# Half-size block products in the two convolutional up stages: seven in place of eight

## The reference

```python
def conv_ffn(h, w_up, conv_w, w_down):
    g, u = jnp.split(dwconv(h @ w_up, conv_w), 2, axis=-1)
    return (jax.nn.silu(g) * u) @ w_down
```

## Time and profile before

| | us |
|---|---|
| median of three runs | 2925.28 |
| the profiled execution, whole | 2923.5 |
| its span in the trace | 2921.7 |
| PE busy | 2722.8 (93% of the span) |
| DVE busy | 575.8 (20%) |
| ACT busy | 356.4 (12%) |
| matmul line of the two up stages (L2830), busy | 455.3 |

### The profile page before, as it was taken

One profiled execution on the slowest core, in us unless ns is written; L12 is line 12 of the kernel. 1 busy time (PEld: TensorE's weight loads), 2 busy tenths in 40 slices (PEclk: granted clock), 3 DMA queues, 4 the chain that ended last, 5 costly groups with the idle time before them and its releaser, 6 DMA issues. The chain is left out here.

```text
span 2921.7 us, 70140 instructions
## 1 busy us (share of the span) xinstructions
PE 2722.8 (93%) x31522; PEld 1995.3 (68%) x31522; DVE 575.8 (20%) x1423; ACT 356.4 (12%) x896; POOL 85.7 (3%) x130
## 2 busy tenths in 40 slices
PE   6889999988899999999998898989999999898999
PEld 3758856658899899999896446865444444555883
DVE  0120001112000000001002224742222201232331
ACT  1010001001000000000002121221111100131110
POOL 0000000000000000000000002200000000000000
PEclk9999999989999999999998999999999999999999
DMA  8663435629999999999991110002222222302432
GB/s 348 258 248 146 156 130 204 257 87 342 364 405 417 392 407 420 411 402 419 400 418 76 43 72 30 3 2 72 79 80 72 72 87 79 119 18 83 148 144 86
DMA packets 80391, 583.94 MB, mean 200 GB/s; under 512 B 8912, under 2 KB 8912, under 8 KB 10064
## 3 DMA queue, kind: packets, MB, share of 16 engines
q1 hardware_dynamic: 79920, 580.15, 50.7%
q10 hardware_dynamic: 288, 1.05, 0.1%
HBM read 580.11 MB, written 1.05 MB: 199 GB/s over the span
## 5 line engine op out<-in xcount | busy, mean ns | idle before, releaser
L1471 PE MATMUL ps<-arena,ring 128*64 128x80 f32 x14336 | 509.5, 234 | 39.1 <-issue 36.1
L1471 PEld LDWEIGHTS ps<-arena,ring 128*64 128x64 f32 x14336 | 503.3, 138 | 44.6 <-issue 42.9
L2830 PE MATMUL ps<-hT,ring 128*128 128x256 f32 (+2 forms) x1472 | 455.3, 472 | 5.6 <-ACT hT L472 3.4
L2830 PEld LDWEIGHTS ps<-hT,ring 128*128 128x128 f32 x1472 | 274.5, 190 | 185.2 <-issue 166.3
L359 PE MATMUL ps<-ring,arena 128*128 128x512 f32 x896 | 390.7, 597 | 4.9 <-DVE arena L2735 3.8
L359 PEld LDWEIGHTS ps<-ring,arena 128*128 128x128 f32 x896 | 171.0, 192 | 218.4 <-issue 212.2
L1480 PE MATMUL ps<-arena,ring 128*64 128x80 f32 x7168 | 255.8, 234 | 19.4 <-issue 19.3
L1480 PEld LDWEIGHTS ps<-arena,ring 128*64 128x64 f32 x7168 | 251.9, 138 | 22.2 <-issue 21.9
L981 PE MATMUL ps<-hT,ring 128*128 128x256 f32 (+1 forms) x736 | 152.7, 370 | 2.6 <-ACT hT L470 2.6
L1621 DVE TENSOR_TENSOR arena<-arena,ps 128x80 f32<-128x80 f32 x224 | 53.2, 237 | 486.9 <-ACT arena L1600 486.8
L981 PEld LDWEIGHTS ps<-hT,ring 128*128 128x128 f32 x736 | 134.8, 190 | 20.3 <-issue 3.0
(11 more groups left out here) (469 smaller groups left out, 2153.5 us busy)
## 6 DMA issues: line engine op xcount, KB each, us to landing
ring<-in_stream SPq DMA_DIRECT2D x547, 1024.0 KB, 7.8
par<-in_params SPq DMA_DIRECT2D x1, 3397.0 KB, 29.3
h<-in_x ACTq DMA_DIRECT2D x2, 512.0 KB, 7.8
cx<-in_ctx SPq DMA_DIRECT2D x2, 512.0 KB, 30.4
out<-h SPq DMA_DIRECT2D x4, 256.0 KB, 2.0
par<-in_params SPq DMA_DIRECT2D x1, 941.0 KB, 5.9
```

The source lines that it names most:

```text
L1471: last = nc.tensor.matmul(ps[m:m + 64, up_bank[j], half * P:half * P + CAP], w[:, k, half * P + m:half * P + m + 64], hTe[:, k, :], start= ...
L2830: last = nc.tensor.matmul(ps[:, 2 * BANKS_CONV[f % RING] + half, tok], w[:, k, half * P:half * P + P], hT[:, k, tok], start=(k == 0), stop ...
```

## The change

The product of a tile is seen as a 2 x 2 block matrix: tokens split into first and second half, input features into low (k 0 to 3) and high (k 4 to 7), columns into left (gate) and right (up). Eight half-size products (half the tokens, half the contraction, half the columns) become seven, with sums of blocks made beforehand and sums of products afterwards, the scheme of Strassen and Winograd:

- Token sums, once for each stage, by DVE (`token_pair`, lines 2903 to 2908 of the kernel after): s1 to s4, from `hT`.
- Weight sums, for each tile, by DVE: t1 and t2 into spare columns of `par`, and two overwrites of the ring's slot (`weight_pair`, L2916 to L2920, and `weight_end`, L2926, which overwrites the block high left once `ab` has read it).
- Seven products of four matmuls each (L2840): `aa` (low left with the first tokens), `ab` (high left with the first tokens), `s1t1`, `s2t2`, `s3t3`, `at4`, `s4b`. `aa`, `s2t2`, `s3t3` and `at4` accumulate on top of each other in one bank; ACT copies the running sum out after each of them (`keep_u1`, `keep_u2`, `keep_u3`, `keep_c21`, L2967), and PE waits for that copy before it adds the next one. `ab`, and `s1t1` with `s4b`, have banks of their own.
- Three additions of a PSUM bank to what ACT kept, by DVE: `c11` (L2932), `c22` (L2938), `c12` (L2944).
- The middle tap (`centre`, L2991), the neighbours (`sides`, L2951 and L2954), silu (L2995) and the product (L2960) are as before, but read the assembled tile in SBUF instead of PSUM.

The products of two tiles are interleaved on PE. `halves_done` and `kept` are one semaphore for each product and each copy. The diff, cut to its core:

```diff
-            def up(pe, f, tok):
-                w = ring[:, (t0 + f) % RING, :].rearrange("p (k n) -> p k n", k=KT)
-                for half in range(2):
-                    for k in range(KT):
-                        last = nc.tensor.matmul(ps[:, 2 * BANKS_CONV[f % RING] + half, tok],
-                                                w[:, k, half * P:half * P + P], hT[:, k, tok],
-                                                start=(k == 0), stop=(k == KT - 1))
...
+            def product(bank, weight, tokens, fresh, end=True):
+                for k in range(kh):
+                    last = nc.tensor.matmul(ps[:, bank, 0:half], weight[:, k, :], tokens[:, k, :],
+                                            start=(fresh and k == 0), stop=(end and k == kh - 1), skip_group_check=True)
                 return last
+            def aa(pe, f):
+                here(pe, f)
+                if f < 2:
+                    claim(pe, bank_a(f))
+                else:
+                    pe.wait_ge(kept["c21"], made(f - 2))
+                product(bank_a(f), tile(f)[:, low, left], hT[:, low, first], True).then_inc(halves_done["aa"], 1)
+            def ab(pe, f):
+                if f < 2:
+                    claim(pe, bank_b(f))
+                else:
+                    pe.wait_ge(c11_made, made(f - 2))
+                product(bank_b(f), tile(f)[:, high, left], hT[:, high, first], True).then_inc(halves_done["ab"], 1)
+            def s1t1(pe, f):
+                if f < 2:
+                    claim(pe, bank_c(f))
+                    pe.wait_ge(token_sums, p0 + 4 * (pairs - 1) + 1)
+                else:
+                    pe.wait_ge(c12_made, made(f - 2))
+                pe.wait_ge(weight_sums, 3 * (c0 + f) + 1)
+                product(bank_c(f), t1[f % 2], s1, True).then_inc(halves_done["s1t1"], 1)
+            def s2t2(pe, f):
+                if f == 0:
+                    pe.wait_ge(token_sums, p0 + 4 * (pairs - 1) + 2)
+                pe.wait_ge(kept["u1"], made(f))
+                pe.wait_ge(weight_sums, 3 * (c0 + f) + 3)
+                product(bank_a(f), t2[f % 2], s2, False).then_inc(halves_done["s2t2"], 1)
+            def s3t3(pe, f):
+                if f == 0:
+                    pe.wait_ge(token_sums, p0 + 4 * (pairs - 1) + 3)
+                pe.wait_ge(kept["u2"], made(f))
+                product(bank_a(f), tile(f)[:, low, right], s3, False).then_inc(halves_done["s3t3"], 1)
...
+            def token_pair(dve, n):
...
+                nc.vector.tensor_tensor(s1[:, :, cols], hT[:, low, s_], hT[:, high, s_], ALU.add).then_inc(token_sums, 1)
+                dve.wait_ge(token_sums, at + 1)
+                nc.vector.tensor_tensor(s2[:, :, cols], s1[:, :, cols], hT[:, low, f_], ALU.subtract).then_inc(token_sums, 1)
+                nc.vector.tensor_tensor(s3[:, :, cols], hT[:, low, f_], hT[:, low, s_], ALU.subtract).then_inc(token_sums, 1)
+                dve.wait_ge(token_sums, at + 2)
+                nc.vector.tensor_tensor(s4[:, :, cols], hT[:, high, f_], s2[:, :, cols], ALU.subtract).then_inc(token_sums, 1)
...
+            def weight_pair(dve, f):
+                here(dve, f)
+                if f >= 2:
+                    dve.wait_ge(halves_done["s1t1"], made(f - 2))
+                    dve.wait_ge(halves_done["s2t2"], made(f - 2))
+                w, n = tile(f), 3 * (c0 + f)
+                nc.vector.tensor_tensor(t1[f % 2], w[:, low, right], w[:, low, left], ALU.subtract).then_inc(weight_sums, 1)
+                dve.wait_ge(weight_sums, n + 1)
+                nc.vector.tensor_tensor(w[:, low, right], w[:, high, right], w[:, low, right],
+                                        ALU.subtract).then_inc(weight_sums, 1)
+                nc.vector.tensor_tensor(t2[f % 2], w[:, high, right], t1[f % 2], ALU.subtract).then_inc(weight_sums, 1)
+            def weight_end(dve, f):
+                w = tile(f)
+                dve.wait_ge(halves_done["ab"], made(f))
+                dve.wait_ge(weight_sums, 3 * (c0 + f) + 3)
+                nc.vector.tensor_tensor(w[:, high, left], w[:, high, left], t2[f % 2], ALU.subtract).then_inc(weight_last, 1)
+            def c11(dve, f):
+                g = gate_c[f % 2][:, first]
+                dve.wait_ge(kept["u1"], made(f))
+                dve.wait_ge(halves_done["ab"], made(f))
+                nc.vector.tensor_tensor(g, g, ps[:, bank_b(f), 0:half], ALU.add).then_inc(c11_made, 1)
...
+            def keep(act, f, name, product_, bank, dst, n):
+                act.wait_ge(halves_done[product_], made(f))
+                if f >= 2:
+                    act.wait_ge(conv_side, 2 * (c0 + f - 2) + n + 1)
+                nc.scalar.activation(dst, ps[:, bank, 0:half], ACT.Copy).then_inc(kept[name], 1)
...
+                for f in range(nf):
+                    if f == 0:
+                        s1t1(pe, 0)
+                        s2t2(pe, 0)
+                        s1t1(pe, 1)
+                    else:
+                        s2t2(pe, f)
+                        if f > 1:
+                            s1t1(pe, f)
+                    s3t3(pe, f)
+                    if 2 <= f + 1 < nf:
+                        aa(pe, f + 1)
+                    at4(pe, f)
+                    if 2 <= f + 1 < nf:
+                        ab(pe, f + 1)
+                    s4b(pe, f)
...
+                for f in range(nf):
+                    keep_u2(act, f)
+                    if f:
+                        silu(act, f - 1)
+                    keep_u3(act, f)
+                    if 2 <= f + 1 < nf:
+                        keep_u1(act, f + 1)
+                    keep_c21(act, f)
+                    centre(act, f, 0)
+                    centre(act, f, 1)
+                silu(act, nf - 1)
...
+                token_pair(dve, pairs - 1)
+                weight_pair(dve, 1)
+                c11(dve, 1)
+                weight_end(dve, 1)
                 for f in range(nf):
-                    b = BANKS_CONV[f % RING]
-                    dve.wait_ge(conv_centre, 2 * (c0 + f + 1))
-                    for half, buf in enumerate((cg, cu)):
-                        x, o = ps[:, 2 * b + half, 0:ntok], buf[:, b, :]
-                        nc.vector.scalar_tensor_tensor(seg(o, 1, SEQ), seg(x, 0, SEQ - 1), tap(0, half, f),
-                                                       seg(o, 1, SEQ), ALU.mult, ALU.add).then_inc(conv_left, 1)
-                    dve.wait_ge(conv_left, 2 * (c0 + f + 1))
-                    for half, buf in enumerate((cg, cu)):
-                        x, o = ps[:, 2 * b + half, 0:ntok], buf[:, b, :]
-                        nc.vector.scalar_tensor_tensor(seg(o, 0, SEQ - 1), seg(x, 1, SEQ), tap(2, half, f),
-                                                       seg(o, 0, SEQ - 1), ALU.mult, ALU.add).then_inc(conv_side, 1)
-                    dve.wait_ge(conv_side, 2 * (c0 + f + 1))
-                    dve.wait_ge(conv_silu, c0 + f + 1)
-                    nc.vector.tensor_tensor(hid[:, f, :], cg[:, b, :], cu[:, b, :],
-                                            ALU.mult).then_inc(conv_hid, 1)
+                    if f:
+                        c12(dve, f - 1)
+                        if f + 1 < nf:
+                            weight_pair(dve, f + 1)
+                        sides(dve, f - 1, 1)
+                    c22(dve, f)
+                    if f:
+                        hidden(dve, f - 1)
+                    if 2 <= f + 1 < nf:
+                        c11(dve, f + 1)
+                        weight_end(dve, f + 1)
+                    sides(dve, f, 0)
```

More of the change, by code:

```diff
@@ L42 @@
 BANKS_PLAIN = [0, 1, 2, 3, 0, 1, 2]
-BANKS_CONV = [0, 1, 2, 0, 1, 2, 1]
 def since(pattern, s):
@@ L2795, in build @@
         (sc_l, sh_l), (sc_c, sh_c) = next_mod
+        halves_done = {name: sem(f"half_{name}") for name in ("aa", "ab", "s1t1", "s2t2", "s3t3", "at4")}
+        kept = {name: sem(f"kept_{name}") for name in ("u1", "u2", "u3", "c21")}
+        weight_sums, weight_last, token_sums = sem("weight_sums"), sem("weight_last"), sem("token_sums")
+        c11_made, c22_made, c12_made = sem("c11_made"), sem("c22_made"), sem("c12_made")
         conv_centre = sem("conv_centre")
+        conv_left = sem("conv_left")
         conv_side = sem("conv_side")
@@ L2801, in build @@
         conv_hid = sem("conv_hid")
[L2802 to L2805 removed]
+        cc = {"n": 0, "pairs": 0}
         def conv_feed_forward(layer, ntok, finish, ready):
[L2808 to L2809 removed]
+            nf, half = F_FFN, ntok // 2
+            segs, ntt = ntok // SEQ, ntok // P
+            pairs = ntt // 2
+            kh = KT // 2
             hid = take(nf, ntok)
             cg, cu = take(3, ntok), take(3, ntok)
[L2812 removed]
+            sums = arena[:, 0:4 * kh * half].rearrange("p (s k t) -> p s k t", s=4, k=kh)
+            s1, s2, s3, s4 = (sums[:, n, :, :] for n in range(4))
```

(90 more changed lines are left out.)

38 lines of the change are left out of this document (21 added, 17 removed).

## The result

The changed kernel took 2892.86 us, median of four runs (2884.24 to 2895.07), against 2925.15 us for the kernel before (four runs, 2924.86 to 2927.46). The ratio is 0.9882, with a 95% interval from 0.9861 to 0.9904: 1.2% faster. The forecast was 2894 us in a range from 2881 to 2908. The profiled execution's span went from 2921.7 to 2889.1 us, 32.6 us less. Everything before the first stage, between the two and behind the second adds up to 2459.7 us in that trace, and to 2459.8 us before, so the whole difference lies in the two stages.

What follows compares the result with a forecast made beforehand. PE was taken as the bound, with DVE having room. First stage 273.3 us (-32.6) and second 157.4 (+1.4) gave -31.2 together: the profiled 2923.5 us became 2892.3, plus 1.8 for the median, 2894 us; range 2881 to 2908.

Steps and rivals of the forecast that it cites:

- The cost of a record by its columns: PE matmul records in both stages: cost in proportion to columns, 0.216 us at 256 and 0.112 us at 128.
- The rival that weight loads come to the front: Second stage: each 128-column record waits for its 192 ns weight load, +90 us, whole kernel 2982 us; chance 5%.
- the prediction's estimate by the Trainium skill: 128-column float32 records with loads, two passes each: 0.162 us, hence 200 us for the second stage, kernel near 2945 us.
- The first stage: PE's 266.1 us of records plus turn, opening, exposed copies and backlog: 273.3 us against 305.9, a gain of 32.6.
- The loop's room there: First stage, per tile: the way from ab to s3t3 takes 4.3 us, PE's three products 5.18, so 0.9 to spare.
- The opening: Start of each stage, after the turn: PE waits 2.7 us for ACT's fills and then DVE's s1.
- The wait for t1 of 0.8 us: Second stage, tile 1: t1 stands behind four token sums on DVE, 0.8 us more.
- The second stage's loop: From ab's end through c11, weight_end, neighbours, c12, centre, keep_u2 to s3t3: 3.24 us against PE's 2.68, 0.56 waiting per tile.
- The clock: Rival: PE's repeated pauses in the second stage lower its clock to 0.94, 9 us more, 2903 us; chance 3%.
- clock at 1.00 in both: Expected sign in the profile after: PE's granted clock stays at 1.00 (2.4 GHz) over both stages.
- the 157.4 us: Second stage's forecast total: 137.6 us of PE records plus waits, including 20 x 0.56 us, against 156.0 before.
- DVE isn't the bound: Second stage: DVE's instructions sum to 5.4 us of a 6.8 us tile, needing a quarter longer to set the pace.

Runs made afterwards that it cites:

- the later centre: Changed kernel with ACT taking centre(f-1, 1) after keep_u2(f) instead of before it, in both stages; 2882.27 us, second stage 146.0 us.

## Why the prediction was right

- **The cost of a record by its columns** was right for both stages: 0.216 us at 256 (243.74 us over 1128 records) and 0.112 at 128, the latter shown in runs of 1112 and 1376. The rival that weight loads come to the front is refuted for such runs. So is, for this case, the prediction's estimate by the Trainium skill, "TensorE: Matmul & The Clock Gate", section "Back-to-back issue gap": 0.162 us, the page's 81 ns per matmul counted twice for a float32 record, where 0.1118 was measured. That tests the doubling and not the page's own 81 ns, as no stream of another type ran here.
- **The first stage**: 273.3 us forecast, 273.1 measured. The loop's room there was put at 0.9 us and measured at 0.93 by adding an instruction.
- **The opening**: 2.7 us forecast; between PE's last record of the turn and `s1t1(0)` it stood idle for 2.6 us (second stage, 2653.76 to 2656.32). The wait for t1 of 0.8 us went when its sums were moved (2.30 us from `s1t1(0)` to `s1t1(1)` against 2.57, one fall of the clock in each).
- **The second stage's loop** was right in its place and its instructions, confirmed by opening it (-10.3 us) and by loading it (+22.7). Its size was a little off: 0.56 us of waiting per tile forecast, 0.45 found (6.70 less 6.25). The last hand-over, ACT to PE with the slower first record, was put at 0.22 us and took 0.16; the copy at 0.28 and took 0.26; several overlaps were 0.01 or 0.02 larger. Over 20 tiles that is 2.2 us.
- **The clock** was a rival at 3% that would cost 9 us, after repeated pauses. It fell, but once, at the opening and not in the steady tiles, whose wait of 0.45 us left it at 1.00; the prediction's sum has no term for that, and its sign "clock at 1.00 in both" didn't hold. The fall cost about 0.9 us: from `s1t1(0)` to `s3t3(0)`, where the order is the same, PE took 4.42 us with it (2656.32 to 2660.74) and 3.55 without it in the first profile of the later centre (2651.86 to 2655.41). So the 157.4 us come nearer to 156.3 than their terms deserve: the loop was put 2.2 us too long, and the missing 0.9 us took part of that back. That is luck, if a small one.
- **DVE isn't the bound**: 5.4 us per tile forecast (5.3 by its own terms), 5.3 measured.

The difference of the whole was forecast at -31.2 us and came out at -32.5 by the stages.

## What to carry to other kernels

- Fewer multiplications pay where the sums between products find room on the other engines; compare, for each copy that a product waits for, the whole way that leads to it in its engine's list with the work that PE has meanwhile. The same code had 0.93 us to spare at 512 tokens and was 0.45 us short at 256.
- A short copy that frees the bound engine should not stand behind a long-awaited instruction in an in-order list. Moving one activation was worth 10 us here and needed no faster engine.
- Add one instruction of known length to the suspected loop, once with the loop closed and once open: +22.7 and +3.8 us tell a loop from an engine that is merely busy.

## What the runs showed of the hardware

- A float32 matmul record of 128 x 128 weights and 128 columns keeps a pitch of 0.112 us over more than 1300 records, though each weight load lasts 0.19 us.
- Waits on semaphores that are met beforehand cost PE nothing that shows here. Each of the seven products of a tile begins with a wait on one or two semaphores, and the first stage's 1128 records keep the pitch of 0.216 us over some 140 such places.
- The granted clock fell to its lower level at the opening of the changed second stage in some executions and not in others. Of the eight traces with the new order there, two have no fall, four have one and two have two; the same program had none and two, which made 2.3 us. One fall in each of the six begins some 1 us after PE's wait of 2.6 us, but the other two lie before it, in the stage's first 32 records. The three traces with the old order, whose wait is 1.7 us, have none. That the wait of 2.6 us brings the falls is therefore not shown.
